# The gate projection of the first attention, with each product split over two 64-row halves of the array

## The reference, cut to what matters

```
def window_attention_mixer(hx, hc, w_in, sink, w_out, need_ctx):
    qx, kx, vx, zx = split_attn(hx @ w_in)
    ...
    ox = window_attention(qx, kx, vx, kc, vc, sink)
    yx = (ox * jax.nn.silu(zx)) @ w_out
```

## Time and profile before

| | |
|---|---|
| median of the runs | 3207.76 us |
| span of the profiled execution (first to last instruction) | 3206.1 us |
| what the median has beyond that span | 1.7 us |
| TensorE busy / weight loads busy | 3133.4 us (98%) / 2569.3 us |
| VectorE / ScalarE / GpSimd busy | 1983.3 / 1635.1 / 112.4 us |
| the gate units (L1683) | 384 matmuls, first at 1452.5, last at 1542.5 us |

### The profile page before, as it was taken

The page is one execution under the profiler, slowest core; times in us unless marked ns, Lnnn a source line. Parts: engine busy times, 40 slices in busy tenths (PEclk is TensorE's granted clock), DMA queues, the critical chain, the costliest instruction groups (busy, mean ns, idle before and its releaser), DMA issues. The chain is left out here.

```text
span 3206.1 us, 43173 instructions
## 1 busy us (share of the span) xinstructions
PE 3133.4 (98%) x17124; PEld 2569.3 (80%) x17124; DVE 1983.3 (62%) x3094; ACT 1635.1 (51%) x2679; POOL 112.4 (4%) x244
## 2 busy tenths in 40 slices
PE   7999999999999999999999999998998999999998
PEld 5988889898888888888787777886687888887886
DVE  7544444445444678742688463446849888878765
ACT  5343443434433457414688453515736777765455
POOL 2000000000000000001000000000000000000000
PEclk9999999999999999999999999999999999999999
DMA  6202011020442567303400541110052222235664
GB/s 216 65 10 86 30 56 60 27 68 22 145 148 96 193 204 257 98 27 85 113 2 2 136 141 53 29 57 27 1 208 88 79 83 88 80 135 187 234 233 150
DMA packets 204921, 322.05 MB, mean 100 GB/s; under 512 B 29339, under 2 KB 117248, under 8 KB 204720
## 3 DMA queue, kind: packets, MB, share of 16 engines
q1 hardware_dynamic: 182800, 241.37, 23.5%
q0 software_dynamic: 20848, 77.85, 7.0%
q10 hardware_dynamic: 1072, 0.07, 0.0%
HBM read 271.97 MB, written 47.28 MB: 100 GB/s over the span
## 5 line engine op out<-in xcount | busy, mean ns | idle before, releaser
L402 DVE TENSOR_TENSOR W_rounded<-W,W_rounded 128x2048 fp32r<-128x2048 f32 (+2 forms) x119 | 201.8, 1696 | 278.4 <-ACT W_rounded L393 275.0
L393 ACT ACTIVATE W_rounded<-W 128x2048 fp32r<-128x2048 f32 (+1 forms) x107 | 168.2, 1572 | 215.0 <-DMA W<-in_ab_w_in 60.2
L4932 PE MATMUL G<-down_ring_rounded 128*128 128x512 f32 x924 | 213.4, 392 | 2.9 <-DVE down_ring_rounded L4995 2.9
L1172 PE MATMUL G<-W_rounded,HT_rounded 128*128 128x512 f32 x640 | 213.7, 415 | 0.0
L2232 PE MATMUL G<-HT_rounded,W_rounded 128*128 128x512 f32 (+1 forms) x768 | 207.8, 355 | 1.6 <-DVE qk_conv L1430 1.6
L1216 PE MATMUL G<-HT_rounded,W_rounded 128*128 128x512 f32 (+1 forms) x768 | 206.6, 355 | 1.0 <-PEq L667 1.0
L4932 PEld LDWEIGHTS G<-down_ring_rounded 128*128 128x128 f32 x924 | 174.2, 189 | 40.3 <-DVE down_ring_rounded L4995 3.8
L3478 PE MATMUL G<-W_rounded,HT_rounded 128*128 128x512 f32 x640 | 201.2, 395 | 0.0
L2232 PEld LDWEIGHTS G<-HT_rounded,W_rounded 128*128 128x128 f32 x768 | 136.6, 188 | 26.6 <-issue 5.2
L1216 PEld LDWEIGHTS G<-HT_rounded,W_rounded 128*128 128x128 f32 x768 | 135.8, 188 | 22.5 <-issue 1.2
L1407 DVE SCALAR_TENSOR_TENSOR c_state<-c_state,decay_all,CC 128x514 f32<-128x514 f32 x64 | 48.0, 750 | 156.9 <-PE CC L1201 156.9
(11 more groups left out here) (627 smaller groups left out, 7805.3 us busy)
## 6 DMA issues: line engine op xcount, KB each, us to landing
up_w_in<-in_w_up SPq DMA_DIRECT2D x44, 512.0 KB, 4.0
W<-in_ab_w_in SPq DMA_DIRECT2D x20, 1024.0 KB, 8.8
W<-in_w_mod SPq DMA_DIRECT2D x8, 2048.0 KB, 8.1
x_rows<-r_xt POOLq DMA_DIRECT2D x32, 512.0 KB, 5.6
down_ring<-act_rows SPq DMA_DIRECT2D x25, 512.0 KB, 4.0
W<-in_c_w_out SPq DMA_DIRECT2D x24, 512.0 KB, 6.8
r_xt<-x_rows POOLq DMA_DIRECT2D x24, 512.0 KB, 4.7
W<-in_w_in SPq DMA_DIRECT2D x12, 1024.0 KB, 5.1
```

What stands on the lines that cost most here:

```text
L393: ins = a.activation(self.half(key, True)[:, at], self.half(key, False, False)[:, at], ACT.Copy)
L402: ins = v.tensor_tensor(self.half(key, False)[:, at], self.half(key, False, False)[:, at], self.half(key, True)[:, at].bitcast(F32), ALU.s ...
L1172: ins = pe.matmul(G[:, K.par(key), :], x[y][:, 4 * kh + k, r * P:(r + 1) * P], wv[z][:, k, :], start=(kh == 0 and k == 0 and (y, z) == SPL ...
L4932: ins = pe.matmul(G[:, bank[r], :], x[y][:, m, r * P:(r + 1) * P], w[z][:, m, :], start=(p in (P1, P5) and q == 0 and m == 0 and (y, z) == ...
```

## The change

Each 128-row matmul of a gate unit becomes two matmuls of 64 rows: inputs 0 to 63 go to one bank and inputs 64 to 127 to another. A gate unit so has two banks: `G` 0 and 1, `G` 2 and 3, or the new pair `GZ`, in turn (z modulo 3). VectorE copies the first bank to a buffer in `q_rows` (`z_sum`), adds the second and frees the pair. ScalarE's sigmoid and VectorE's product (`gated`, one unit later than the sum) read the buffer. POOL's store waits for the product through its own semaphore. TensorE enters unit z when unit z - 3 has been summed; units 0 and 1 take the banks of jobs 24, 25 and 22, 23 and wait until these are read. The attention's start waits also for the sum of unit 14, whose banks its scores take. In the last pair both products of VectorE come as `gated(14)`, `first_scores`, `gated(15)`.

```diff
+    GZ = K.ps(st, "GZ", [P, 2, 512])
+    s_zm, ZM = s_in, 16
+    def halves(z):
+        return GZ if z % 3 == 2 else G[:, 2 * (z % 3):2 * (z % 3) + 2, :]
+    def z_sum(z):
+        return qr[:, 2 + z % 2, :]
     def read(eng):
         eng.wait_ge(s_tqr, len(jobs))
+        K.wait_read(eng, gates[-2])
@@ gpsimd
-            K.wait_read(g, key)
+            g.wait_ge(s_zm, ZM + n + 1)
@@ gate_unit
+            pair = halves(gates.index(key))
             for k in range(4):
                 for y, z in SPLIT_PASSES:
-                    ins = pe.matmul(bank(key), w[y][:, k, m * P:(m + 1) * P], x[z][:, 4 * kh + k, rc * 512:(rc + 1) * 512],
-                                    ...
+                    for b in range(2):
+                        rows_of = slice(64 * b, 64 * b + 64)
+                        ins = pe.matmul(pair[:, b, :], w[y][rows_of, k, m * P:(m + 1) * P],
+                                        x[z][rows_of, 4 * kh + k, rc * 512:(rc + 1) * 512],
+                                        ...
@@ tensor
-                    if kh == 0:
+                    if kh == 0 and stage[0] == "az":
+                        z = gates.index(key)
+                        for old in {0: jobs[-2:], 1: jobs[-4:-2], 2: []}.get(z, gates[z - 3:z - 2]):
+                            K.wait_read(pe, old)
+                    elif kh == 0:
                         K.wait_bank(pe, key, 4)
-                        if stage[0] != "az":
-                            rows.ready(pe, key[-1] + 1)
+                        rows.ready(pe, key[-1] + 1)
@@ scalar
-                    K.wait_unit(a, key)
+                    K.wait_read(a, key)
-                    ch.link(a.activation(e, bank(key), ACT.Relu, bias=K.cut[:, :]))
+                    ch.link(a.activation(e, z_sum(z), ACT.Relu, bias=K.cut[:, :]))
@@ vector
+        def gated(v, z):
+            v.wait_ge(s_ez, z + 1)
+            v.tensor_tensor(ez[:, z % 4, :], z_sum(z), ez[:, z % 4, :], ALU.mult).then_inc(s_zm, 1)
+                    K.wait_unit(v, key)
+                    if z < 2:
+                        v.wait_ge(s_tq, len(jobs) - 2)
+                    if z >= 2:
+                        v.wait_ge(s_zm, ZM + z - 1)
+                    ch.link(v.tensor_copy(z_sum(z), halves(z)[:, 0, :]))
+                    K.free_bank(v.tensor_tensor(z_sum(z), halves(z)[:, 1, :], z_sum(z), ALU.add), key)
+                    if z >= 1:
+                        gated(v, z - 1)
                     if j == 2 * len(pairs) - 1:
                         K.first_scores(v)
-                    v.wait_ge(s_ez, z + 1)
-                    K.free_bank(v.tensor_tensor(ez[:, z % 4, :], bank(key), ez[:, z % 4, :], ALU.mult), key)
+                        gated(v, z)
```

More of the change, by code:

```diff
@@ L1680, in gate_unit @@
             _, half, m, rc = key
+            pair = halves(gates.index(key))
             for k in range(4):
                 for y, z in SPLIT_PASSES:
-                    ins = pe.matmul(bank(key), w[y][:, k, m * P:(m + 1) * P], x[z][:, 4 * kh + k, rc * 512:(rc + 1) * 512],
-                                    start=(kh == 0 and k == 0 and (y, z) == SPLIT_PASSES[0]),
-                                    stop=(kh == 1 and k == 3 and (y, z) == SPLIT_PASSES[-1]))
+                    for b in range(2):
+                        rows_of = slice(64 * b, 64 * b + 64)
+                        ins = pe.matmul(pair[:, b, :], w[y][rows_of, k, m * P:(m + 1) * P],
+                                        x[z][rows_of, 4 * kh + k, rc * 512:(rc + 1) * 512],
+                                        start=(kh == 0 and k == 0 and (y, z) == SPLIT_PASSES[0]),
+                                        stop=(kh == 1 and k == 3 and (y, z) == SPLIT_PASSES[-1]), skip_group_check=True)
             return ins
```

## The result

| | before | after |
|---|---|---|
| median of the runs (us) | 3208.22 (3207.66 to 3209.14, 4 runs) | 3224.17 (3223.43 to 3225.81, 4 runs) |
| ratio to before | | 1.0049, 95% interval 1.0037 to 1.0060 |
| span of the profiled execution (us) | 3206.1 | 3222.1 |

The change makes the kernel 16 us slower. The forecast was 3221.0 us in a range of 3214 to 3231.

The account below looks back on a forecast made before the run. TensorE, busy 98% of the span, was taken to bound the kernel. Entry wait 7.1 + second wait 4.2 - pace 2.8 + clock 3.1 + tile shape 0.1 + end 1.5 = 13.2 us, so 3207.8 becomes 3221.0 us; range 3214 to 3231.

Parts of the forecast that it names:

- Pace: Gate matmuls: a pair of 64-row halves takes 224 ns against 232 a product, 2.8 us gained over 348 products.
- Entry wait: Ahead of unit 0, TensorE waits 7.1 us until VectorE, behind its half of item 7's split, has read job 25.
- Second wait: Ahead of unit 9, TensorE waits for unit 6's sum behind item 9's split: 4.65 less 0.45, 4.2 us lost.
- Clock: Half clock for 3.42 us behind each new wait loses 1.6 us, 3.1 in all; bounds 0 and 6.2.
- Tile changes: Switches between 128-row and 64-row products, at the transposes of jobs 24 and 25 and the end: +0.1 us.
- Sums, stores, buffers: VectorE's 16 copies and 16 sums, 22 us, and POOL's later stores cost nothing; under 1 us if late at unit 5.
- End: After unit 15, VectorE's copy and sum delay the last product and POOL's copies; attention starts 1.5 us late, bounds 1.2 and 2.
- A slow pair (260 or 464 ns): Rival 1: gate halves hinder each other or run serially; 3234 or 3304 us; chance 0.07, of it 0.03 serial.
- the pair at 236 ns: Skill's rule for packed tiles, about 4 ns more for each further tile: gate pair at 236 ns, 3225 us.
- A pair faster than its columns: Rival 2: gate halves stream faster than a column per cycle, under 213 ns; 3183 us at 116 ns; chance 0.04.
- The waits were not cheap: Rival 3 claimed cheap waits: pair at 213 ns, no low clock behind either wait, +6.3 us, 3214.1 us; chance 0.06.
- slower: Chance that the kernel measures slower: forecast and rival 1, with a third of rival 3's neighbourhood, given as 0.89.

Follow-up runs that it names:

- The lone half: Changed kernel with both waits removed and the second 64-row half of every gate product left out, VectorE adding the first bank twice: 3243.6 us, one run.
- the single edits: Changed kernel with unit 0 given GZ and unit 2 the job banks: 3217.73 us; or with VectorE's split of item 9 behind unit 6's sum: 3220.64 us.
- The last experiment: Changed kernel with both waits removed, and the attention's first maxima taken ahead of unit 14's product: 3210.60 us, ratio 1.0006.

## Why the prediction was right, step by step

- *Pace.* Here the forecast was off. It took 224 ns, midway between 216 and 232, and put 2.8 us of gain into the sum; the pairs take 232 ns and the gain is nothing. With 232 the same sum is 16.0 us, which is what was measured. That it agrees so closely is luck in part: the second wait, the tile changes and the end are off by 0.2 to 0.4 us each, and 0.9 us come back behind the attention that the sum doesn't have. The forecast named 232 as possible, and its row spoke for it: at half clock 128-row products have no excess over their columns, so the 19 ns appear only at full clock. A limit of each partition's own stream, which halving the rows leaves alone, would fit that, but no run shows it to be the reason. The lone half at 232 ns shows that halves neither hinder nor help. The two-cycle pairs at 0.43 ns per column and cycle were no guide to the one-cycle form at 0.45.
- *Entry wait.* Forecast 7.1 us, gap 7.1, start 7.3 later within the stage (VectorE's split itself came some 0.1 later relative to the stage). Shown twice: it goes when unit 0 takes other banks, and it comes alone in the kernel of 128-row products.
- *Second wait.* Forecast 4.65 less 0.45; measured 5.1 less 0.5. The load landed 7.8 us behind the release instead of 7.3. Shown by moving the split behind unit 6's sum.
- *Clock.* Forecast 1.6 us behind each wait; 1.6 and 1.6 in the changed kernel's trace. In others the half clock lasted 5.6 to 6.1 us behind the same waits, 2.6 to 2.8 us each, inside the bounds given. So 1.6 is the low end of what such a wait cost here, and that both waits of the profiled run show it is partly luck. That variation is about half of why the single edits gained less than expected (1.2 of 2.4 us and 1.0 of 2.2); the rest isn't explained.
- *Tile changes.* Forecast 0.1 us in all; 0.3 are seen at the transposes (pair 13's last block and they take 3.47 instead of 3.14 us), less 0.1 at the end, where the first scores now start 0.23 us behind the last gate product instead of 0.33.
- *Sums, stores, buffers.* Free as forecast: no wait inside the stage is ended by a sum except the one priced at unit 9.
- *End.* Forecast 1.5 us for the attention's start, measured 1.2. POOL's copies and the exponentials behind them are 1.5 later relative to the last product, as forecast. But in the changed kernel TensorE doesn't wait for them. It waits 3.06 us for the maxima instead of 1.64, then computes two sets of scores that half clock stretches (1.93 and 2.08 us against 1.15 each), and goes from these to the transposes without a wait; before it waited 1.11 us there for the scaled exponentials. The first scaled exponentials are ready at 1567.6, the transposes start at 1568.0: the two paths end within 0.4 us of each other, so the trace doesn't say what either alone would cost. The last experiment speaks for the other bank order only.
- *Later stages.* 0.9 us come back behind the attention. The forecast had nothing for it and no run isolates it. In the profiles of the other kernels the same stretch gave from 0.3 us back to 3.8 lost (the run without the second wait), so it stays open whether the change has a part in it.
- *Rivals.* A slow pair (260 or 464 ns) is out by the pace. So is the pair at 236 ns, though its 3225 us lies nearer to the measured time than the forecast's. A pair faster than its columns is out too. The waits were not cheap: both had half clock behind them.
- *Slips that change nothing.* "1.1 us in two places" is one wait counted twice, of the matmul and of the weight load. And the parts of "slower" (0.83, 0.07 and a third of 0.06) make 0.92, not 0.89.

No version here beats the kernel before: the best, with both waits removed and the maxima moved, is at 1.0006 (0.9997 to 1.0015).

## What to carry to other kernels

Before splitting a product to use the array otherwise, ask whether the excess over the column rate belongs to the rows or to the stream; one lone half, read from a stretch at full clock, answers it. When banks are dealt out anew, take for each new owner the last reader of the bank and what that engine has queued ahead of the read: both waits here came from a weight split that stood in front of a bank read, where nobody had waited before. Price a wait of several us at its length plus the half clock behind it (here 1.6 to 2.8 us).

## What the runs showed of the hardware

- A stream of lone 64-row products, with no more than 0.42 us of idle time in it, lost the full clock after 54 us and did not get it back in the remaining 66 us; entered at half clock, it stayed there for 165 us (one run each). Pairs of 64-row products, at the same 232 ns a product, kept 1.00.
- One-cycle products of 512 columns: 232 ns with 128 rows, with a pair of 64 rows, and with 64 rows alone; 427 ns at half clock, where no excess is left. 64 stationary columns, or the same parts each time, give 227.
- Weight loads of 64 x 128 took 184 ns against 188 for 128 x 128; with 64 columns 134. A load 54 ns shorter takes 5 ns off the pace, so its length is at most 5 of the 19 ns.
